# Second attention of a two-block network: convolution gates around one weight remainder, pooling in two parts, the last token blocks in another order

## The reference

```
p = rms_norm(x) @ w_in           # q, k, v (8 heads of 64), gb, gc, hin (256 each), u (256)
y_attn = banded attention over q, k, v with a relative bias
z = gc * hin
y_conv = gb * sum(conv_w[i] * z shifted by 2 - i rows)          # 3 taps
m = (mean of the last 2, 4, 8 or 16 rows of u) - u              # one window per 64 channels
y_pool = (m @ pool_w[g]) * pool_scale
x = x + concat(y_attn, y_conv, y_pool) @ w_out                  # 1024 x 1024
```

## Time and profile before

| | |
|---|---|
| median of 3 runs | 1451.44 us (1448.82 to 1452.07) |
| the profiled execution | 1446.65 us |
| its span, first to last instruction | 1444.9 us |
| mean granted clock of TensorE | 0.991 |
| PE busy | 1375.4 us (95%), 6567 matmuls |
| DVE busy | 690.8 us (48%) |
| POOL busy | 687.7 us (48%) |
| ACT busy | 546.9 us (38%) |

### The profile page before, as it was taken

The page is one execution under the profiler, slowest core; times in us unless marked ns, Lnnn a source line. Parts: engine busy times, 40 slices in busy tenths (PEclk is TensorE's granted clock), DMA queues, the critical chain, the costliest instruction groups (busy, mean ns, idle before and its releaser), DMA issues.

```text
span 1444.9 us, 17281 instructions
## 1 busy us (share of the span) xinstructions
PE 1375.4 (95%) x6567; PEld 1126.3 (78%) x6567; DVE 690.8 (48%) x1005; ACT 546.9 (38%) x793; POOL 687.7 (48%) x544
## 2 busy tenths in 40 slices
PE   2999999999999999999999988998899999999999
PEld 2887787788777778888888877876678888888887
DVE  6676978788744672131316356247413214132131
ACT  0636454577653253232322334225324224133231
POOL 0553855333346664454455554825344544544442
PEclk9999999999999999999999999999999999999999
DMA  9343345654324333223222322251122232223222
GB/s 330 113 137 93 94 146 171 201 148 134 98 71 145 119 88 117 87 87 116 87 89 86 115 88 88 88 146 46 43 88 88 88 115 89 87 92 111 87 92 82
DMA packets 132248, 158.58 MB, mean 110 GB/s; under 512 B 9468, under 2 KB 93712, under 8 KB 131936
## 3 DMA queue, kind: packets, MB, share of 16 engines
q1 hardware_dynamic: 123760, 146.95, 32.3%
q10 hardware_dynamic: 6240, 5.40, 1.6%
q0 software_dynamic: 2192, 5.49, 1.2%
HBM read 153.47 MB, written 2.26 MB: 108 GB/s over the span
## 4 chain that ended last, share of the span: by engine, by line
PE 82%; DVE 9%; POOL 3%; issue 3%; ACT 2%; DMA 1%; SPq 0%; DVEq 0%; POOLq 0%; ACTq 0%
PE bank L1694 25%; PE bank L1696 24%; PE bank L1695 24%; POOL w_lo L546 3%; DVE tmp L1267 2%; PE bank L1829 1%; DMA arena<-in_w_ada_dram 1%; ACT w_hi L740 1%; PE bank L1960 1%; DVE rinv L1174 1%; PE bank L1814 1%; PE bank L2196 1%; PE bank L1839 1%; PE bank L2016 1%; DVE arena L1192 1%
## 5 line engine op out<-in xcount | busy, mean ns | idle before, releaser
L546 POOL TENSOR_TENSOR w_lo<-raw,w_hi 128x512 fp32r<-128x512 f32 x428 | 584.5, 1397 | 619.1 <-ACT w_hi L740 617.9
L1694 PE MATMUL bank<-w_hi,a_hi 128*128 128x512 f32 x928 | 367.2, 396 | 22.7 <-POOL w_lo L546 9.8
L1695 PE MATMUL bank<-w_lo,a_hi 128*128 128x512 f32 x928 | 363.9, 392 | 0.0
L1696 PE MATMUL bank<-w_hi,a_lo 128*128 128x512 f32 x928 | 363.9, 392 | 0.0
L740 ACT ACTIVATE w_hi<-raw 128x2048 fp32r<-128x2048 f32 x107 | 204.7, 1913 | 363.6 <-PE bank L1696 360.1
L1694 PE MATMUL bank<-a_hi,w_hi 128*128 128x512 f32 x800 | 316.4, 396 | 3.4 <-DVE a_lo L1160 2.5
L1696 PE MATMUL bank<-a_hi,w_lo 128*128 128x512 f32 x800 | 312.5, 391 | 0.0
L1695 PE MATMUL bank<-a_lo,w_hi 128*128 128x512 f32 x800 | 312.5, 391 | 0.0
L1694 PEld LDWEIGHTS bank<-w_hi,a_hi 128*128 128x128 f32 x928 | 176.0, 190 | 61.8 <-issue 12.3
L1696 PEld LDWEIGHTS bank<-w_hi,a_lo 128*128 128x128 f32 x928 | 175.8, 189 | 37.4
L1695 PEld LDWEIGHTS bank<-w_lo,a_hi 128*128 128x128 f32 x928 | 176.3, 190 | 36.0
(11 more groups left out here) (248 smaller groups left out, 1251.0 us busy)
## 6 DMA issues: line engine op xcount, KB each, us to landing
raw<-in_w_mlp_dram SPq DMA_DIRECT2D x32, 1024.0 KB, 5.2
raw<-in_w_in_dram SPq DMA_DIRECT2D x24, 1024.0 KB, 5.2
arena<-in_w_ada_dram SPq DMA_DIRECT2D x18, 1024.0 KB, 6.5
raw<-in_w_ff_in_dram SPq DMA_DIRECT2D x16, 1024.0 KB, 5.4
raw<-in_w_ff_out_dram SPq DMA_DIRECT2D x16, 1024.0 KB, 5.0
raw<-in_w_out_dram SPq DMA_DIRECT2D x12, 1024.0 KB, 6.0
raw<-in_w_in_dram SPq DMA_DIRECT2D x16, 512.0 KB, 5.7
arena<-in_w_ada_dram SPq DMA_DIRECT2D x3, 2048.0 KB, 18.0
```

Source lines behind the costliest of these rows:

```text
L546: last = pool.tensor_tensor(w_lo[:, u0 % 2, cols], raw[:, u0 % 2, cols], w_hi[:, u0 % 2, cols].bitcast(F32), ALU.subtract)
L1694: pe.matmul(out_, hi_a, hi_b, start=start, stop=False)
L1695: pe.matmul(out_, hi_a, lo_b, start=False, stop=False)
L1696: return pe.matmul(out_, lo_a, hi_b, start=False, stop=stop)
```

## The change

- POOL: `gate_conv(0)` stands in front of `lo(U_WO3)` and no longer behind it; `gate_conv(1)` stays behind.
- ACT: in each step `copy_probT` stands in front of `fetch_inverse`. `mix_hi(2)` moves from step 7 to the end of step 6, `mix_hi(3)` from the middle of step 8 to its start. `hi(U_WO3 + 1)` moves from behind the loop into step 8, in front of `send_inverse`.
- DVE: `pooling` is cut into `window_sums` and the halves. The whole of tile 0 moves from behind step 0's maxima to behind `read_cp(0)`; tile 1's sums move from step 1 to in front of step 0, its halves from step 1 to the end of step 0. `mix_lo(2)` moves from step 7 to the end of step 6, `mix_lo(3)` from step 8 to step 7, in front of the bias and maxima of the last head.
- TensorE: the blocks of `mix_rows` go 3, 2, 0, 1 in place of 3, 0, 1, 2. Block 2 waits only for the first two exponentials of the last head. The row half of the attention channels waits pair by pair for `band_lo`.

```diff
@@ POOL
             short_conv(1)
+            gate_conv(0)
             lo(U_WO3)
-            gate_conv(0)
             gate_conv(1)
@@ ACT, steps
             for s in range(10):
+                if s == 8:
+                    mix_hi(3)
                 if s >= 2:
+                    copy_probT(16 + s - 2, prob2T)
                     fetch_inverse(16 + s - 2)
-                    copy_probT(16 + s - 2, prob2T)
...
-                elif s in (7, 8):
-                    mix_hi(s - 5)
-                if s in (2, 5):
+                if s in (2, 5, 8):
                     hi(U_CP + s // 3 + 3)
                 if 1 <= s < 9:
                     send_inverse(16 + s - 1)
                 if s in (4, 6, 8):
                     band_high(s // 2 - 2)
+                if s == 6:
+                    mix_hi(2)
             band_high(3)
-            hi(U_WO3 + 1)
@@ DVE
+            def window_sums(n):
+                src, at_ = cp[:, 6 + n], 0
+                for lag in (1, 2) if n == 0 else (1, 2, 4, 8):
+                    dst = cp[:, at_]
+                    link(dve.tensor_copy(dst[:, 0:lag], src[:, 0:lag]))
+                    link(dve.tensor_tensor(dst[:, lag:], src[:, lag:], src[:, 0:S - lag], ALU.add))
+                    src, at_ = dst, 1 - at_
...
             read_cp(0)
+            dve.wait_ge(cp_read, 1)
+            window_sums(0)
+            pooling(0)
...
+            dve.wait_ge(cp_read, 2)
+            window_sums(1)
             for s in range(10):
...
-                elif s in (7, 8):
-                    mix_lo(s - 5)
...
                 if s >= 2:
                     output(16 + s - 2)
+                if s == 7:
+                    mix_lo(3)
                 if s < 8:
...
-                if s < 2:
-                    dve.wait_ge(cp_read, s + 1)
-                    pooling(s)
+                if s == 0:
+                    pooling(1)
+                elif s == 6:
+                    mix_lo(2)
@@ TensorE
-                if t in (0, 2):
+                if t in (2, 1):
                     last.then_inc(ticks, 1)
...
                 elif s == 9:
-                    pe.wait_ge(p_made, 4 * 24)
                     mix_rows(0)
...
+                if s == 8:
+                    pe.wait_ge(p_made, 4 * 23 + 2)
+                    mix_rows(2)
...
             mix_rows(1)
-            mix_rows(2)
-            pe.wait_ge(o_made, 24)
-            pe.wait_ge(band_lo, 4)
-            row_half(U_WO3, 1, 1, 1, 0, False, True)
+            row_half(U_WO3, 1, 1, 1, 0, False, True, ready=band_lo)
```

More of the change, by code:

```diff
@@ L1471, in pool_counts @@
                 link(dve.reciprocal(pinv[:].rearrange("p a b -> p (a b)"), pinv[:].rearrange("p a b -> p (a b)")))
-            def pooling(n):
[L1475 to L1493, removed]
@@ new lines, in window_sums @@
+            def window_sums(n):
[5 more added lines that the diff above has]
+                    src, at_ = dst, 1 - at_
+            def pooling(n):
+                u = cp[:, 6 + n]
+                for po, place, w in ((0, 0, 2 if n == 0 else 8), (64, 1, 4 if n == 0 else 16)):
+                    h = slice(po, po + 64)
+                    link(dve.tensor_tensor(cp[h, place, 0:16], cp[h, place, 0:16], pinv[h, n], ALU.mult))
+                    link(dve.tensor_tensor(u[h, 0:16], cp[h, place, 0:16], u[h, 0:16], ALU.subtract))
+                    ins = dve.scalar_tensor_tensor(u[h, 16:], cp[h, place, 16:], 1.0 / w, u[h, 16:], ALU.mult, ALU.subtract)
+                    if po:
+                        ins.then_inc(m_made, 1)
+                        dve.wait_ge(m_made, n + 1)
+                    else:
+                        link(ins)
@@ L1734, in column_pair, with row_half @@
                     column_tile(u0 + j // 2, j % 2, act_buf, bank[4 * s + j][:], None, i, per)
-            def row_half(u0, b, s, act_buf, kk0, first, final, wait=None, i=0, per=0):
+            def row_half(u0, b, s, act_buf, kk0, first, final, wait=None, i=0, per=0, ready=None):
                 slot = (u0 + b) % 2
@@ L1745, in row_half @@
                         pe.wait_ge(a_lo_made, wait(kk))
+                    if ready is not None and t == 0:
+                        pe.wait_ge(ready, kk + 1)
                     a = slice(P * t, P * t + P)
```

## The result

The changed kernel took 1435.7 us (median of 6 runs, 1432.70 to 1441.72), the kernel before 1450.13 us (6 runs, 1446.48 to 1452.07). The medians are 14.4 us apart. The ratio, which goes by the means, is 0.9913, with a 95% interval from 0.9884 to 0.9941: faster by 0.9%, or 12.6 us. In the profiled executions the span went from 1444.9 to 1432.2 us, 12.7 us less. The forecast was 11.5 us less for the profiled execution and 1439.9 us for the runs.

What follows compares the result with a forecast made beforehand. TensorE, busy 95% of the span, bounds the kernel; idle time and lower clock in the second attention allow 19.1 us. Head +1.4 and tail +10.1 give 11.5 us: 1435.1 profiled, 1439.9 for runs, range 1432.5 to 1444.5 (own 1437.5 to 1442.5).

Steps and rivals of the forecast that it cites:

- The bound of 19.1 us: Second attention: the most the change could win, 13.4 us of TensorE idle time plus 5.7 us of lower clock.
- Collision at step 0, 3.1 us late: Head: DVE's second-tile sums collide with POOL's weight split, so step 0's addition starts 3.1 us later than 964.10.
- Head, +1.4 us: Head of the loop: 5.4 us won, 3.1 given back, about 0.9 of lower clock after the new wait.
- Swapped fetches are hidden: Steps 2 to 9: fetches issued some 1.4 us later still land before the outputs that need them.
- First block right behind the transposes: Tail: the first block follows without a gap, so the 6.01 us wait and the 2.3 us behind it go.
- New wait at step 9, 2.45 us: Tail: TensorE's last two transposes wait 2.45 us for DVE's output of head 6; bounds 1.7 and 3.0 us.
- The slow stretch behind it, 1.2 us: Tail: lower clock after the new wait for DVE's output at step 9, 0 to 1.7 us, taken as 1.2.
- The 3.25 us wait goes with the moved split: Tail: the weight split is ready at 1040.3, so the 3.25 us wait and 1.7 us behind it go.
- no collision: Rival, step 0: DVE and POOL don't collide, 15.5 us won, 1436.0 us; chance 13%.
- late fetches: Rival, steps 2 to 9: swapped fetches land late and make the kernel slower, about 1456 us at 8 us; chance 3%.
- The clock does not fall: Rival, head and tail: no lower clock after the two new waits, 13.6 us won, 1437.8 us; chance 15%.
- late step 7 chain: Rival, step 7: DVE holds up the last weight split or gate_conv(1); 4 to 8 us left, about 1445; chance 10%.

Runs made afterwards that it cites:

- e10: Changed kernel, but ACT splits U_WO3 + 1 at the end of step 8 and POOL waits for the second tile's whole pooling; ratio 0.9878 against before.
- e1: Changed kernel, but POOL waits with its split of unit U_CP + 2 until DVE has done the second tile's sums; ratio 0.9897 against before.
- e7: Kernel before with only the fetch of the inverse put behind the three copies in ACT's order; ratio 0.9992 against before.
- e6: Changed kernel with POOL's gate_conv(0) behind the split of U_WO3 again; ratio 0.9919 against before.
- e2: Changed kernel, but ACT splits U_WO3 + 1 at the end of step 8, behind send_inverse and band_high(2); ratio 0.9909 against before.
- e4: Changed kernel with the pooling back in steps 0 and 1, the swap of fetch and copy kept; ratio 0.9950 against before.
- e8: Changed kernel with ACT's split of U_WO3 + 1 behind the loop and band_high(3) again; ratio 0.9951 against before.
- e3: Kernel before with only the pooling moved and the fetch put behind the copy; ratio 1.0009 against before.
- e9: Changed kernel with token block 2 last again (3, 0, 1, 2); ratio 0.9916 against before.

## Why the prediction was right

- **The bound of 19.1 us** (idle time plus clock losses). e10 reaches 18.9, so the accounting of what bounds this part holds; 0.46 us of wait are left in it.
- **Collision at step 0, 3.1 us late.** Right in place, and e1 removes it: 967.21 for 967.2, a wait of 2.92 for 3.1 us. That the time fits so well is partly luck. The second sum was done at 965.32 and not at 964.3, since the copy in front of it was blocked too, and the last two pairs, which ran after POOL's split, took 1.8 us and not 2.9; the two errors cancel. POOL was done at 964.8 and not at 965.6: it lost only 0.45 us by the collision (5.43 against 4.98), so it is DVE that pays. The Trainium skill ("SBUF — State Buffer", "Who interferes with whom") says that copies in a two-port mode can contend as well; the trace agrees for the 128x2 copy, 1.11 us beside POOL against 0.17. The 128x1 copy took 0.14 us, but it started at 960.60, just as POOL passed from its first part to its second, so it decides nothing. The sum that I had worked out from that rule, 0.4 us later still, did not come true, because the last two pairs met no split any more.
- **Head, +1.4 us.** It was 1.0. The slow stretch behind the new wait cost 1.7 us (3.50 us at 0.51), not 0.9. The two small waits go by the swap, as I said, but their 1.2 us count only once the pooling has moved: in e7 the next wait grew by as much.
- **Swapped fetches are hidden.** Right in e7 and in the changed kernel, where no output waits for a DMA. The cover is not large, though: in e6, where the fetch of one step was issued 1.7 us later, the output waited 0.68 us for it.
- **First block right behind the transposes.** Right, 6.01 us and the 2.3 behind it are gone. The last addition starts 0.93 us behind the start of the transposes (1026.83 and 1025.90) and not 0.59 (1027.53 and 1026.94), which is the 0.3 us that I had for it.
- **New wait at step 9, 2.45 us.** It was 2.16, with both causes as described (e2). **The slow stretch behind it, 1.2 us,** is the term that was mis-sized: 0 in the profile after, 1.7 in e4. That is most of the difference between +10.1 and 11.7 us for the tail, and it is luck: with e4's clock the tail would be worth 10.0.
- **The 3.25 us wait goes with the moved split.** Right (e8).
- **The sum, 11.5 us.** It was 12.7, with the head 0.4 too high and the tail 1.6 too low. The clock makes it less sure than it looks: by the 1.7 us that such a stretch costs, I estimate that the same waits could have given 11.0 (a stretch at step 9 too, as in e4) or 14.4 us (none in the head, as in e6).
- **The figure for runs, 1439.9 us.** It was 4.2 us too high. The median of 1435.7 lies in the wide range (1432.5 to 1444.5) but below my own of 1437.5 to 1442.5. Of the error, 1.1 us come from the sum (1435.1 against 1433.96) and 3.1 us from the 4.8 us that I added for the gap between the profiled execution and the median, which was 1.7 here. My figure for "no collision", 1436.0, lies nearer to the median, though e1 shows the collision.
- **The rivals.** No collision and late fetches are out (e1, e7). "The clock does not fall" came true for the second new wait and not for the first. The late step 7 chain did not occur in the changed kernel; in its nearest trial, e6, the last remainder is late and the whole costs 1.6 us, so it was priced too high.

What stays open is whether a given wait of 2 to 3 us will be followed by the lower clock.

## What to carry to other kernels

Before moving work into an engine's idle time, look at what the neighbour engine does in that very stretch: the hole was nearly long enough (3.43 us for 3.7), and yet the work took 6.6 us there. When the neighbour's work has slack, as POOL's split had 20 us of it (done at 964.8, used at 984.9), let the neighbour wait; one semaphore was worth 3.9 us, of which 1.7 were lower clock. And in a queue that runs in order, a long instruction that is moved forward delays every short one that it overtakes. Put it behind the short ones that others wait for, as e2 did: the gain stays, and of the 2.16 us wait that it had caused 0.47 are left.

## What the runs showed of the hardware

- **The clock after short waits isn't settled by the wait's length.** After the 2.9 us wait in the head TensorE's clock fell in the changed kernel (0.51 over 3.50 us) and in e2, e3, e8 and e9 (0.52 to 0.57 over 3.50 us), and it stayed at 1.00 for 7.60 us in e6. After the wait at step 9 it stayed at 1.00 in the changed kernel (2.16 us), in e1 (2.17 us) and in e6 (2.24 us), and fell to 0.59 in e4 (2.15 us).
- **The same instructions ran at two clocks in the first block.** In e1's profile, in three stretches long before anything that was changed, TensorE ran at 0.77, 0.80 and 0.89; in the profile of the changed kernel it had 1.00 in the same stretches. e1, then the changed kernel:

```profile
185.00:200.00 15.00, 13.81 (x60) 0.77 0.44 142
245.00:262.00 17.00, 14.62 (x57) 0.80 0.86 249
280.00:295.00 15.00, 13.39 (x70) 0.89 0.58 161
```

```profile
185.00:200.00 15.00, 13.82 (x75) 1.00 0.39 128
245.00:262.00 17.00, 14.70 (x73) 1.00 0.68 201
280.00:295.00 15.00, 13.91 (x84) 1.00 0.72 204
```

  That is 15 x 0.23 + 17 x 0.20 + 15 x 0.11 = 8.5 us, and e1's first scores stand 8.0 us later. The timed runs of the changed kernel fall into two groups as well: four from 1432.7 to 1436.8 us at a mean clock of 0.993 to 0.995, two at 1441.2 and 1441.7 us at 0.989 and 0.988. e7's profile is a second case: it has 0.77, 0.90 and 1.00 in the same stretches, its first scores stand at 966.09, and its mean clock is 0.987. That this is what makes the intervals of the ratios 0.5% wide is likely but not shown, since only profiled executions tell where the clock was lost.
